# Token gates as rounded one-hot rows and two single products, with ScalarE making the low rows

## The reference

```python
idx = jnp.take_along_axis(cand_idx, pos, axis=-1)      # 128 * first + second
gate = jax.nn.softmax(s_fin, axis=-1)
act = gelu(einsum('thkd,td->thk', u[idx], x)) * gate
y = einsum('thk,thkd->td', act, v[idx])
```

## Time and profile before

| | |
|---|---|
| runs of the program | 3044.01, 3045.37, 3046.30 us; median 3045.37 us |
| profiled execution, its own time | 3049.36 us |
| span of the profiled execution | 3047.6 us (1.8 us lie around it) |
| stage of the change (slots 28 to 63 of peer_u0) | about 1696.5 to 1963.5 us of the span |
| granted TensorE clock, mean of the span | 0.992 |
| PE busy | 2976.6 us |

### The profile page before, as it was taken

How to read it: one execution, slowest core, us unless ns; L and a number is a source line. 1 busy time by engine, 2 the same in 40 slices (tenths; PEclk the granted TensorE clock), 3 DMA queues, 4 the chain that set the end, 5 groups by cost and what they waited for, 6 DMA issues and landing times.

```text
span 3047.6 us, 46827 instructions
## 1 busy us (share of the span) xinstructions
PE 2976.6 (98%) x18947; PEld 2686.6 (88%) x18947; DVE 1750.3 (57%) x2414; ACT 1255.5 (41%) x1501; POOL 44.9 (1%) x62
## 2 busy tenths in 40 slices
PE   7999999999999999999999999999999999999998
PEld 6887899999997889777899999988889999988887
DVE  5555555554555555675898778644444444444444
ACT  4334444444334334444344444444443333334444
POOL 0000022000000000000000000000000000000000
PEclk9999999999999999999999999999999999999999
DMA  5556433335545454334545555555556655555554
GB/s 208 195 205 228 171 140 122 128 132 172 180 165 193 152 193 152 127 137 165 177 172 191 173 170 172 176 194 193 193 193 234 236 183 186 182 180 193 193 194 178
DMA packets 90215, 542.88 MB, mean 178 GB/s; under 512 B 9328, under 2 KB 25840, under 8 KB 26352
## 3 DMA queue, kind: packets, MB, share of 16 engines
q1 hardware_dynamic: 70992, 513.94, 47.9%
q10 hardware_dynamic: 19104, 27.27, 2.5%
HBM read 530.68 MB, written 10.49 MB: 178 GB/s over the span
## 4 chain that ended last, share of the span: by engine, by line
PE 89%; DVE 6%; ACT 3%; issue 1%; DMA 0%; ACTq 0%; DVEq 0%; SPq 0%
PE bank L499 33%; PE bank L987 23%; PE bank L512 9%; PE bank L594 8%; PE bank L516 5%; PE bank L569 3%; DVE wlo L1671 2%; ACT whi L1035 2%; PE bank L767 2%; PE bank L634 1%; PE bank L965 1%; PE bank L724 1%; DVE R L2308 1%; DVE hT L1661 0%; PE bank L709 0%
## 5 line engine op out<-in xcount | busy, mean ns | idle before, releaser
L1671 DVE TENSOR_TENSOR wlo<-raw,whi 128x2048 fp32r<-128x2048 f32 (+1 forms) x484 | 1104.0, 2281 | 1120.3 <-ACT whi L1035 1119.4
L1035 ACT ACTIVATE whi<-raw 128x2048 fp32r<-128x2048 f32 (+1 forms) x484 | 921.2, 1903 | 1258.1 <-PE bank L987 410.5
L499 PE MATMUL bank<-hT,whi 128*128 128x256 f32 x6400 | 1194.5, 287 | 2.8 <-DVE xres L2373 1.7
L499 PEld LDWEIGHTS bank<-hT,whi 128*128 128x128 f32 x6400 | 996.0, 192 | 5.9 <-issue 3.4
L499 PE MATMUL bank<-hT,wlo 128*128 128x256 f32 x3200 | 905.8, 283 | 0.0
L499 PEld LDWEIGHTS bank<-hT,wlo 128*128 128x128 f32 x3200 | 612.7, 191 | 0.0
L512 PE MATMUL bank<-hT,whi 128*128 128x512 f32 x1280 | 447.6, 398 | 3.0 <-DVE wlo L1671 3.0
L516 PE MATMUL bank<-hT,wlo 128*128 128x256 f32 x1280 | 344.8, 281 | 1.3 <-DVE wlo L1671 1.3
L512 PEld LDWEIGHTS bank<-hT,whi 128*128 128x128 f32 x1280 | 236.2, 188 | 57.4 <-issue 6.6
L987 PE MATMUL bank<-whi,ghi 128*128 128x512 f32 x1016 | 272.2, 390 | 3.7 <-DVE glo L2379 3.7
L987 PE MATMUL bank<-wlo,ghi 128*128 128x512 f32 x1016 | 272.4, 390 | 0.0
(11 more groups left out here) (322 smaller groups left out, 1978.9 us busy)
## 6 DMA issues: line engine op xcount, KB each, us to landing
raw<-stream SPq DMA_DIRECT2D x484, 1024.0 KB, 4.8
R<-cmpw ACTq DMA_DIRECT2D x8, 1024.0 KB, 5.8
gates_dram<-R ACTq DMA_DIRECT2D x64, 128.0 KB, 4.9
R<-gates_dram ACTq DMA_DIRECT2D x16, 512.0 KB, 5.1
xres<-x SPq DMA_DIRECT2D x2, 1024.0 KB, 6.1
R<-mixw ACTq DMA_DIRECT2D x1, 1024.0 KB, 6.9
R<-fnw ACTq DMA_DIRECT2D x1, 1024.0 KB, 5.6
raw<-fnw SPq DMA_DIRECT2D x1, 1024.0 KB, 4.8
```

The source lines that it names most:

```text
L499: last = mm(bank[b][:, t * T:(t + 1) * T], w[t][:, ks], x_[:, k, :], start=(at == 0 and n == 0), stop=(at == KC - 1 and n == 2))
L1035: A(whi[t][:, 0:w], raw[t][:, 0:w], ACT.Copy).then_inc(hi_ready[t], 1)
L1671: V.tensor_tensor(wlo[t][:, 0:w], raw[t][:, 0:w], whi[t][:, 0:w].bitcast(F32), ALU.subtract).then_inc(raw_free[t], 1)
```

## The change

`second_hot` and `first_hot` are now written as fp32r, so that the gate in a first row is rounded. What the rounding loses is put in third rows, `low_hot`: ACT makes them from the first rows, times a factor of the token and choice, ratio = (gate - rounded gate) / rounded gate. The product of a token becomes two fp32r matmuls of 128 columns with the same stationary operand, summed in the bank. PE waits for `low_ready` in place of `hot_ready`. In slots with one group its tokens now come after k = 9, 11, 13, 15 instead of k = 3, 7, 11, 15; in slots with two groups they stay at the odd k. Before the stage ACT rounds the gates (`gate_hi`), and DVE computes `ratio` in four instructions of 128 x 256.

```diff
+        rounded_hot = nc.alloc_sbuf_tensor_at("rounded_hot", [P, 2 * TRACK * NK], F32R, offset=R_base + 4 * (sc_at + 768))
+        rounded_low = nc.alloc_sbuf_tensor_at("rounded_low", [P, TRACK * NK + T], F32R, offset=R_base + 4 * (sc_at + 4608))
+        first_hot, second_hot = (rounded_hot[:, a:a + TRACK * NK].rearrange("p (t n) -> p t n", n=NK)
+                                 for a in (0, TRACK * NK))
+        low_hot = rounded_low[:, 0:TRACK * NK].rearrange("p (t n) -> p t n", n=NK)
+        gate_hi = rounded_low[:, TRACK * NK:TRACK * NK + T]
+        gate_lo = region(sc_at + 5632 + T, T)
+        ratio = region(sc_at + 5632 + 2 * T, T)
...
             def token_gates(groups, k):
-                every = KC // (4 * len(groups))
-                if k % every == every - 1:
-                    n, c = divmod(k // every, 4)
+                n, c = divmod(k // 2 - (4 if len(groups) == 1 else 0), 4)
+                if k % 2 == 1 and n >= 0:
                     m = groups[n]
                     if c == 0:
                         pe.wait_ge(g_kept, m + 1)
                         pe.wait_ge(g_weighted, m + 1)
-                        pe.wait_ge(hot_ready, m + 1)
+                        pe.wait_ge(low_ready, m + 1)
                     at = (4 * m + c) % TRACK
-                    last = mm(bank[4 + m % 4][:, c * P:(c + 1) * P], second_hot[:, at, :], first_hot[:, at, :],
-                              start=True, stop=True)
+                    mm(bank[4 + m % 4][:, c * P:(c + 1) * P], second_hot[:, at, :], first_hot[:, at, :],
+                       start=True, stop=False)
+                    last = mm(bank[4 + m % 4][:, c * P:(c + 1) * P], second_hot[:, at, :], low_hot[:, at, :],
+                              start=False, stop=True)
...
                     last.then_inc(chosenT_copied, 1)
+                    act.wait_ge(chosenT_copied, 1)
+                    A(gate_hi, idxT[:, 2, :], ACT.Copy).then_inc(gate_high, 1)
...
+            def low_rows(m):
+
+                if m == 0:
+                    act.wait_ge(ratio_ready, 1)
+                act.wait_ge(hot_ready, m + 1)
+                for t in range(4):
+                    at = (4 * m + t) % TRACK
+                    last = A(low_hot[:, at, :], first_hot[:, at, :].bitcast(F32), ACT.Copy,
+                             scale=ratio[:, 4 * m + t:4 * m + t + 1])
+                last.then_inc(low_ready, 1)
+
             act.sem_inc(g_kept, 4)
+            for m in range(2):
+                low_rows(m)
...
                 for m in groups_of(slot):
                     keep_gates(m, known_acts(slot))
+                    if m + 2 < T // 4:
+                        low_rows(m + 2)
...
             for m in range(2):
                 hot_rows(m)
+            dve.wait_ge(gate_high, 1)
+            step(V.tensor_scalar(ratio, gate_hi.bitcast(F32), 1e-30, None, ALU.max))
+            V.tensor_tensor(gate_lo, idxT[:, 2, :], gate_hi.bitcast(F32), ALU.subtract)
+            step(V.reciprocal(ratio, ratio))
+            V.tensor_tensor(ratio, ratio, gate_lo, ALU.mult).then_inc(ratio_ready, 1)
```

More of the change, by code:

```diff
@@ L201, in build_two_blocks @@
         par = sb("par", [P, n_params])
+        R_base = nc.sbuf_base
         R = sb("R", [P, R_WORDS])
@@ L294, in build_two_blocks @@
         idxT = region(sc_at, 768).rearrange("p (s t) -> p s t", s=3)
-        first_hot = region(sc_at + 768, TRACK * NK).rearrange("p (t n) -> p t n", n=NK)
-        second_hot = region(sc_at + 1792, TRACK * NK).rearrange("p (t n) -> p t n", n=NK)
+        rounded_hot = nc.alloc_sbuf_tensor_at("rounded_hot", [P, 2 * TRACK * NK], F32R, offset=R_base + 4 * (sc_at + 768))
[6 more added lines that the diff above has]
+        ratio = region(sc_at + 5632 + 2 * T, T)
         staged = region(sc_at + 2816, 512).rearrange("p (a k) -> p a k", a=2)
@@ L370, in build_two_blocks @@
             "mo_sig", "cells", "head_sq", "head_ms", "head_rt"))
+        gate_high, ratio_ready, low_ready = sem("gate_high"), sem("ratio_ready"), sem("low_ready")
         (qs_ready, qs_copied, gate_arg, gate_exp, chosen_ready, chosenT, chosenT_copied) = (
```

## The result

The changed kernel takes 3116.8 us, median of four runs (3111.4 to 3120.1), against 3045.2 us for the kernel before (with a fourth run; three gave 3045.4); the ratio is 1.0234, with an interval of 1.0216 to 1.0251. Forecast were 3113.8 us. The change costs 71.6 us where 68.4 were worked out.

The account below looks back on a forecast made before the run. PE is busy 98% overall, but in the stage an ACT and DVE loop (7.33 us, 7.87 with gelu) rivals PE's slot. Loop growth 28.1 + 32.0 + 3.8 and start 4.5 add 68.4 to 3045.4: 3113.8 us, range 3084 to 3136.

Parts of the forecast that it names:

- The bound: Stage slots: ACT and DVE loop 7.33 us (7.87 with gelu) against PE's 7.45; PE at its limit in 14 of 29.
- The price of a low row: ACT's four new 128 x 128 instructions per group: 0.29 us each, bounds 0.18 and 0.40.
- The loop: ACT and DVE in two-group slots: from 7.33 to 9.46 us, 10.00 with a gelu; chance 0.80.
- The stall of PE: PE in each slot: two chunks, then 2.4 us waiting for low rows; busy share in the stage near 75%.
- The start: Before slot 30: four DVE instructions at 0.43 us and eight low rows put its start 4.5 us later.
- The pair of products: PE, per token: two single products take 0.13 us for the float32 product's 0.21; bounds 0.12 and 0.42.
- 20 us for what PE could save: PE, all 256 tokens: 256 x 0.08 us saved by pairs at 0.13, if PE set the pace.
- The clock: Rival: PE's stalls halve the clock; up to 3.5 us per slot hidden, 7 us costs 23, giving 3137; chance 0.07.
- The sum: Whole stage: 28.1 and 32.0 us for two-group slots, 3.8 for one-group slots, 4.5 for the start, together +68.4 us.

## Why the prediction was right

- *The bound.* That the stage hangs on a loop of ACT and DVE of 7.33 us is shown from both sides: taking 27 us from PE gave 4, and taking the gelu out of the loop gave 5 with nothing taken from PE. It held more than the prediction said: PE was to be at its limit in the 14 slots with two groups and no gelu, but there too one product for two left the 7.33 to 7.47 us as they were.
- *The price of a low row.* 0.29 was taken; four rows occupy 1.19 (1739.71 to 1740.90), 0.30 each. The slope of ACT and two far rows gave it.
- *The loop.* 9.46 and 10.00 were summed; between DVE's splits lie 9.40 (1735.56 to 1744.96) to 9.43 and, with a gelu, 9.93 to 10.02 in all but five slots with two groups, and 7.34 to 7.38 and 7.81 to 7.84 in slots with one group (7.27 and 7.81).
- *The stall of PE: right in kind, too large.* Two chunks and a wait, as laid out; that it is a symptom and not the cause is shown by the run in which PE does not wait for the low rows. But 2.4 us in each slot and a busy share near 75% were forecast. There are 24 waits for the low rows, from 0.16 to 2.6 us, and PE is busy for 283 of the 331.5 us from 1696.5 to 2028, 85%. The clock filled the gap: after a stall the granted clock often fell to 0.50 for 3 us or more, PE took longer over the same products, and the next stall was shorter.

```profile
1741.14 0.30 PE L972 MATMUL bank<-rounded_hot 128*128 128x128 f32 x1 [2.24 <-ACT rounded_low L1517]
...
1744.00:1745.00 1.00, 1.00 (x6) 0.50 0.03 5
...
1750.54 0.30 PE L972 MATMUL bank<-rounded_hot 128*128 128x128 f32 x1 [0.16 <-ACT rounded_low L1517]
```

  The middle line is a window of PE (length, busy, then the granted clock).
- *The start.* 4.5 us were forecast on 0.43 for each of DVE's four instructions. The reciprocal took four times that:

```profile
1694.24 0.43 DVE L2351 TENSOR_TENSOR R<-R,rounded_low 128x256 f32<-128x256 f32 x1
1694.58 1.75 DVE L2352 RECIPROCAL R<-R 128x256 f32<-128x256 f32 x1
1696.36 0.42 DVE L2353 TENSOR_TENSOR R<-R 128x256 f32<-128x256 f32 x1
```

  The sum was too small here by 1.3 us. From the last split ahead of the stage to PE's first product of slot 30 it was 17.3 us before (1692.34 to 1709.63) and 23.2 after (1687.70 to 1710.88): 5.9 more, where 4.5 were forecast.
- *The pair of products: wrong.* I took 0.13 us from the 0.14 between two starts in rows 6; it is 0.21 to 0.22. Those rows hold one float32 product of 15 columns (x2, its two records) and then one of 256, not two short ones. The price of such a short product shows in what follows: the 256 columns of L695 behind it took 0.51 us from start to start (375.93 to 376.44), the same columns of L696 behind L695 only 0.44. The kernel before had the price in plain sight: its float32 product of 128 columns leaves two records, each with a weight load of its own (512 for 256 tokens), and costs 0.21. The Trainium skill ("TensorE: Matmul & The Clock Gate", LDWEIGHTS: columns / 1.2 ns, 107 ns for 128) gave the right number, and the runs agree with it: 0.11 for one product and 0.21 for two. That the weight load is what sets this price is argued and not shown, as no run has a stationary operand of another width; a fixed price of a short product would look the same here. The step failed without harm, since the prediction had worked out that up to 0.42 would be hidden; but its 20 us for what PE could save should have been zero. The change as it stands could not win anything on PE: 0.21 us of a float32 product became 0.21 us of two fp32r ones.
- *The clock.* Priced as hidden up to a point, with 0.07 for more. It fell to 0.92 in the stage, mostly hidden as said under the stall, but PE was late five times; in this timeline of DVE the second `weigh` of a slot waits for a token's product:

```profile
1744.96 2.29 DVE L1697 TENSOR_TENSOR wlo<-raw,whi 128x2048 fp32r<-128x2048 f32 x1 [3.45 <-ACT whi L1044]
...
1749.66 0.29 DVE L2342 TENSOR_TENSOR R<-bank,R 128x128 f32<-128x128 f32 x1 [0.58 <-PE bank L974]
...
1754.73 2.29 DVE L1697 TENSOR_TENSOR wlo<-raw,whi 128x2048 fp32r<-128x2048 f32 x1 [3.15 <-ACT whi L1044]
```

  That loop is 9.77 where its neighbour is 9.40. The five (9.77, 10.23, 9.86, 10.46 and 10.49) add 2.7 us in this execution. In each DVE waits for PE, 0.57 to 1.00 us, and ahead of each the granted clock was 0.50 for 3 to 7 us. The run in which PE does not wait for the low rows has a clock of 0.90 to 0.98 in its windows of 50 us too, but only one late loop (9.19 for 7.25 in slot 29, behind 6.5 us at 0.50): here a stretch at half clock costs time only where PE is then late. The four runs of the changed kernel fit this: the two slower ones (3119.0 and 3120.1) have a mean clock of 0.983, the two faster ones (3114.6 and 3111.4) 0.987 and 0.988.
- *The sum: near, with some luck.* From the last split of DVE ahead of the stage to the first behind it lie 273.96 us in the profile before (to 1966.30) and 343.88 in the profile after (to 2031.58), 69.9 more where 68.4 were summed. The start was 1.4 us too small and the five late loops, 2.7, were not in the sum. The rest was 2.6 too large: most loops came out at 9.40 to 9.43 and 9.93 to 9.96 instead of 9.46 and 10.00, and those with a gelu before at 7.86 to 8.02 instead of 7.87. These errors cancel in part. What lies between 69.9 and the 71.6 of the medians is inside the spread of the four runs.

## What to carry to other kernels

Ask of each engine's work in a stage whether it stands in a loop with another engine's, and how long the loop is, before asking which engine is busiest: ACT was 41% busy, and of the 2.4 us per slot that were given to it 2.1 came out at the end (7.33 to 9.40), because its idle time was waiting inside the loop. Here the loop was cured by order and depth, not by speed: what the next split does not need goes behind it, and rows are made a slot ahead. And price a short product by a whole pattern of products, with and without it, not by the distance of two starts: one float32 product of 128 moving columns cost 0.21 us here, and so did the two fp32r ones in its place.

## What was not expected of the hardware

- A product of 128 moving columns costs 0.11 us and not half of the 0.12 of 256 columns, although its start and the next one's are only 0.06 apart: the delay shows in the products behind it.
- A reciprocal on DVE took 1.75 us for 256 columns, where a product of two tensors of that size took 0.42.
- Idle stretches of PE of up to 2.6 us, in loops of 9.4 to 10 us, brought the granted clock to 0.90 to 0.93 in four of six windows of 50 us (0.96 and 0.97 in the other two), by stretches at 0.50 (1.2 GHz of 2.4); 1.4 us of products in the wait of each slot with two groups brought it back to 0.97 or more.
